# Two chained transformer blocks on one core: moved waits, a reordered opening and first norm, earlier masks, a variance beside a GEMM, the result written by chunk, and a rotary sum moved to POOL

## Chip, cores and metric

One core of one Trainium2 chip runs the whole kernel. The metric is the device time of one execution in microseconds (us), lower is better. The kernel before took 3072.14 us, the median of three runs from 3069.19 to 3078.15.

## What is computed

The input is one sequence of 256 tokens of width 1024 in float32, and the output has the same shape. Two models run one after the other:

```
h = first_block(x, c, ctx, c_ctx, ...)   # 2 layers: FFN, mixer, FFN; each norm scaled and shifted by rows made from c
    layer 0: swiglu(1024 -> 2*2816 -> 1024); retention over x and 256 context tokens; swiglu
    layer 1: swiglu; neighbourhood attention (NAT), 16 heads of 64, bias, softmax over 512 keys; w_o; swiglu
out = second_block(h, ...)               # 2 layers
    proj = rms_norm(x) @ w_in            # 1024 -> queries, keys, values of three attentions, and gates
    oa = rms_norm(diff_attention) * c    # 4 heads, two softmaxes each
    ob = moba_attention                  # 4 heads of 128
    oc = mla_attention                   # 8 heads of 64 + 32 rotary dimensions
    x += rms_norm(sum(sigmoid(gates) * branches) @ w_out)
    x += rms_norm(square(relu(rms_norm(x) @ w_up)) @ w_down)
```

## The kernel before

**Tiling.** Activations stand transposed, channels on the 128 partitions and 256 tokens (512 with the context) along the row. Every weight matrix is streamed from memory once, in blocks of 128 rows by up to 2048 columns per channel group, into six `raw` slots. For float32 accuracy each product is made of three: the weight is split into `w_high`, rounded by ScalarE (ACT, L1004), and `w_low`, the rest, by VectorE (DVE, L1478), and the input into a high and a low half in the same way. TensorE (PE) multiplies high by high, low by high and high by low (L2168). A block is split in two instructions on each engine, and three `w_high` slots exist. A weight block gives one or two chunks of output in PSUM, and four `gemm` banks take them in turn.

**Order.** Nothing is scheduled by a tool. There is one straight program for each engine, and each runs a list of stages of the same names (`ffn`, `norm_in_halves`, `gemm`, `attention`, `update_and_open`). The engines meet at semaphores only. What stands in an engine's queue behind a waiting instruction waits too.

**Attention beside GEMMs.** `attention` is a generator of steps: `scores` (L2320, bias added at L2324), row maximum (DVE, L1702), exponentials (ACT, L1187), division by the sum (DVE, L1721), `turn` (the transposes of the probabilities, L2345 for NAT and L2353 elsewhere, copied out by ACT at L1197 or L1201), and `values` (L2373, out by ACT and DVE at L1207 and L1729). `alongside` sets GEMM chunks between these steps: at step x it has let through `upto` of them. All three engines read the same table:

```python
for x in range(2 * len(a.pairs) + 1):
    next(steps)
    upto = {"nat": min(24, x - x // 13), "dif": (x + 1) // 2, "mob": min(4, 1 + (x + 1) // 2),
            "mla": x + (x + 1) // 2}[a.kind]
```

**Norms.** A norm needs squares (ACT), their sums over partitions by a product with ones (PE, `added_squares` L2093, `mean_square` L2082), a root (ACT), its inverse (DVE, L1510), and the inverse spread over the partitions (PE, L2109). Only then the input of the next GEMM is made (DVE, L1529 and L1516). `norm_in_halves` does it within the last groups of a GEMM (`tail`). `update_and_open` adds a normed output to `h` and opens the next GEMM, and the squares of `h` are taken beside it.

**Queues besides.** SyncE (SP) issues the weight loads in order of use, and POOL has small work: sums of squares (L937), copies of the rotary keys (L974), additions of the branches (L982).

**Names in the rows.** `tt` is the NAT bias with its mask, `mq` and `mk` are the MLA queries and keys, `pexp` the probabilities, `act_high`/`act_low` the split outputs or mixes, `nat_high`/`nat_low` the NAT output, `yt` a temporary, `yh`/`yl` the split normed input. `wide` in `gemm` means that the first two blocks are multiplied row by row of the input as it comes, instead of chunk by chunk.

## Time and profile before

| | us |
|---|---|
| median of 3 runs (lowest, highest) | 3072.14 (3069.19, 3078.15) |
| profiled execution, its own time | 3069.35 |
| its span in the trace | 3067.5 |
| PE busy | 2976.7 |
| DVE busy | 1822.4 |
| ACT busy | 1175.9 |
| POOL busy | 166.7 |

PE is busy for 97% of the span. The mean granted clock of PE was 0.987 of full speed. The rest of the span, 90.8 us, is some fifty waits of PE. In the profile `PE aux L2320 <- ACT pexp L1187` reads: TensorE stood idle before its instruction at line 2320, and what came last of the things it waited for was ScalarE's write of `pexp` at line 1187.

### The profile page before, as it was taken

How to read it: one execution, taken by the hardware profiler on the slowest of the kernel's cores; microseconds unless marked ns; L12 is line 12 of the kernel's file. 1: busy time of each engine (PE TensorE's matmuls, PEld its weight loads, DVE VectorE, ACT ScalarE, POOL GpSimd, SP SyncE). 2: the span in 40 equal slices, each digit the busy share in tenths (PEclk: the TensorE clock that was granted, in tenths of full speed). 3: DMA queues.
4: the chain of work that ended last, by engine and by line, in shares of the span. 5: the costliest groups of instructions: out<-in, count | busy, mean ns of one | idle time of the engine just before them, and what ended most of it. 6: DMA issues, size and time to landing. Idle time of an engine off the chain costs nothing. (4 is left out here: it accounts for less than half of the span.)

```text
span 3067.5 us, 46310 instructions
## 1 busy us (share of the span) xinstructions
PE 2976.7 (97%) x19019; PEld 2647.2 (86%) x19019; DVE 1822.4 (59%) x3378; ACT 1175.9 (38%) x2019; POOL 166.7 (5%) x199
## 2 busy tenths in 40 slices
PE   7999999999999999999999998999999999999998
PEld 4888889888888888888888778999898999899998
DVE  4777775443569886743334445556656656656665
ACT  4222224333342222332223344444544544455453
POOL 2000010000010000100001110000002001001100
PEclk9999999999999999999999999999999999999999
DMA  7556552222236565632324324656335554435452
GB/s 231 151 165 185 158 163 92 73 69 83 69 95 186 185 195 175 194 88 84 110 71 126 92 78 111 186 167 191 97 118 185 165 185 137 138 97 172 152 185 91
DMA packets 509004, 421.42 MB, mean 137 GB/s; under 512 B 18235, under 2 KB 505963, under 8 KB 508793
## 3 DMA queue, kind: packets, MB, share of 16 engines
q1 hardware_dynamic: 505752, 412.33, 43.8%
q0 software_dynamic: 3040, 6.13, 0.8%
q8 instruction: 151, 2.47, 0.3%
q14 instruction: 61, 0.49, 0.1%
HBM read 417.30 MB, written 1.12 MB: 136 GB/s over the span
## 5 line engine op out<-in xcount | busy, mean ns | idle before, releaser
L1478 DVE TENSOR_TENSOR w_low<-raw,w_high 128x1024 fp32r<-128x1024 f32 (+2 forms) x720 | 765.3, 1104 | 321.0 <-ACT w_high L1004 319.8
L1004 ACT ACTIVATE w_high<-raw 128x1024 fp32r<-128x1024 f32 (+2 forms) x720 | 648.6, 950 | 648.6 <-PE gemm L2168 308.1
L2168 PE MATMUL gemm<-xh,w_high 128*128 128x512 f32 (+1 forms) x1904 | 688.4, 362 | 5.1 <-DVE xl L1516 4.5
L2168 PE MATMUL gemm<-xl,w_high 128*128 128x512 f32 (+1 forms) x1904 | 680.9, 358 | 0.0
L2168 PE MATMUL gemm<-xh,w_low 128*128 128x512 f32 (+1 forms) x1904 | 680.8, 358 | 0.0
L2168 PEld LDWEIGHTS gemm<-xh,w_high 128*128 128x128 f32 x1904 | 359.7, 189 | 62.0 <-issue 5.6
L2168 PEld LDWEIGHTS gemm<-xh,w_low 128*128 128x128 f32 x1904 | 359.2, 189 | 57.3
L2168 PEld LDWEIGHTS gemm<-xl,w_high 128*128 128x128 f32 x1904 | 359.6, 189 | 55.5 <-issue 0.2
L2168 PE MATMUL gemm<-yh,w_high 128*128 128x256 f32 x1216 | 350.7, 288 | 12.8 <-DVE yl L1541 7.1
L2168 PE MATMUL gemm<-yl,w_high 128*128 128x256 f32 x1216 | 345.5, 284 | 0.0
L2168 PE MATMUL gemm<-yh,w_low 128*128 128x256 f32 x1216 | 344.9, 284 | 0.0
L1449 DVE SCALAR_TENSOR_TENSOR macc<-raw,sc,macc 128x256 f32<-128x256 f32 x812 | 337.6, 480 | 4.0
L2168 PE MATMUL gemm<-hid_high,w_high 128*128 128x512 f32 (+1 forms) x770 | 272.2, 354 | 0.0
L2168 PE MATMUL gemm<-hid_low,w_high 128*128 128x512 f32 (+1 forms) x770 | 269.1, 350 | 0.0
L2168 PE MATMUL gemm<-hid_high,w_low 128*128 128x512 f32 (+1 forms) x770 | 269.1, 349 | 0.0
L2168 PE MATMUL gemm<-act_high,w_high 128*128 128x256 f32 (+1 forms) x888 | 253.3, 285 | 6.7 <-DVE yt L1671 6.7
L2168 PE MATMUL gemm<-act_low,w_high 128*128 128x256 f32 (+1 forms) x888 | 250.8, 282 | 0.0
L2168 PE MATMUL gemm<-act_high,w_low 128*128 128x256 f32 (+1 forms) x888 | 250.7, 282 | 0.0
L2168 PEld LDWEIGHTS gemm<-yh,w_high 128*128 128x128 f32 x1216 | 232.9, 192 | 16.2 <-issue 14.6
L2168 PEld LDWEIGHTS gemm<-yl,w_high 128*128 128x128 f32 x1216 | 233.0, 192 | 0.2
L2168 PEld LDWEIGHTS gemm<-yh,w_low 128*128 128x128 f32 x1216 | 232.7, 191 | 0.0
L1647 DVE TENSOR_TENSOR hf<-sq,gemm 128x512 f32<-128x512 f32 (+1 forms) x88 | 54.6, 620 | 266.6 <-PE gemm L2168 266.6
(335 smaller groups left out, 4230.1 us busy)
## 6 DMA issues: line engine op xcount, KB each, us to landing
raw<-in_ffn_w_in SPq DMA_DIRECT2D x176, 512.0 KB, 5.2
raw<-in_w_mod SPq DMA_DIRECT2D x72, 1024.0 KB, 7.6
raw<-in_w_in SPq DMA_DIRECT2D x50, 1024.0 KB, 5.3
raw<-in_w_up SPq DMA_DIRECT2D x32, 1024.0 KB, 5.4
raw<-in_w_down SPq DMA_DIRECT2D x32, 1024.0 KB, 5.0
raw<-in_ffn_w_out SPq DMA_DIRECT2D x32, 768.0 KB, 4.6
raw<-in_ret_w_in SPq DMA_DIRECT2D x24, 1024.0 KB, 5.2
raw<-in_ffn_w_out SPq DMA_DIRECT2D x32, 640.0 KB, 4.0
```

The source lines that it names most:

```text
L1004: act.activation(wh[i % SPL][:, a:b], raw[slot_of["w", i]][:, a:b], ACT.Copy).then_inc(w_high, 1)
L1449: dve.scalar_tensor_tensor(out=acc, in0=raw[slot][:, WB * k:WB * k + WB], scalar=sc[:, k, v:v + 1], in1=acc, op0=ALU.mult, op1=ALU.add).th ...
L1478: dve.tensor_tensor(wl[slot][:, a:b], raw[slot][:, a:b], wh[i % SPL][:, a:b].bitcast(F32), ALU.subtract).then_inc(w_low, 1)
L1647: dve.tensor_tensor(hf[:, pr % 2, 0:tok], sa[:, pr % 2, 0:tok], ps[:, 0:tok], ALU.mult).then_inc(odd_free, 1)
L2168: ins = pe.matmul(out, l_, r_, start=first and j == 0, stop=last and j == 2)
```

## The change

These edits are made, none of which changes a number that is computed:

1. **Opening.** SP loads the rows of `x` and `ctx` after three `w_mod` blocks instead of four. PE transposes them before the modulation rows of block 2, and turns and rows of the last blocks stand behind the sums of squares. ACT takes the root, and DVE the inverse, earlier. DVE makes the first two input pieces before the second weight block's low half.
2. **`norm_in_halves`.** In `tail` the sums come 3·nt+2 products into the second half (8 or 14) instead of 6, and the spread 14 or 16 instead of 10.
3. **Masks.** DVE adds the mask to the first four heads' bias ahead of the GEMM `nat_v0` instead of behind it.
4. **`alongside`.** The tables differ by a chunk here and there. MOBA and MLA attention run as one sequence of pairs with one table. The last four steps of NAT let through pieces of the output GEMM `nat_o` on PE, by the new parameter `ahead` (which groups, from which row, to which row).
5. **`mixed{l}`** multiplies rows 0 to 5 of both first blocks, chunk by chunk, before it waits for the last two mixes.
6. **Rotary sums.** The eight additions `mq = yt + yt` of each layer go from DVE (L1990) to POOL, behind the key copies. The MLA scores wait for them, and so do ACT's squares that reuse `yt`.
7. **`update_and_open`.** DVE divides the next piece before it makes the last one's low half, in another order than before for the first two.
8. **Variance.** PE's sums of squares for `mlp_pre` come behind the third group of `up{l}0`, and the squares go to `pexp2` instead of `yt`.
9. **Result.** The final transposes start with each pair of channel groups that is ready, into the four GEMM banks. ACT copies them out in four pieces instead of DVE in eight, and four half-width stores replace two.

```diff
@@ -209,7 +209,7 @@
-        out_buf = [rows_of[:, D * t:D * t + D] for t in range(2)]
+        out_buf = rows_of[:, 0:2 * D].rearrange("p (t n) -> p t n", t=2)
@@ -469,6 +469,8 @@
+            if N["name"][:7] == "mlp_pre":
+                N["buf"] = N["buf"][:3] + (pexp2,)
@@ -775,21 +778,21 @@
-        def alongside(name, steps, rest, lag=0):
+        def alongside(names, steps, rest):
...
-            for x in range(2 * len(a.pairs) + 1):
+            for x in range(2 * sum(len(atts[name].pairs) for name in names) + 1):
...
-                upto = {"nat": min(24, x - x // 13), "dif": (x + 1) // 2, "mob": min(4, 1 + (x + 1) // 2),
-                        "mla": x + (x + 1) // 2}[a.kind]
-                while done < upto - lag:
-                    next(rest)
+                upto = {"nat": min(24, 1 + x - x // 13) + (x >= 28) + (x >= 29) + (x >= 30) + (x >= 32), "dif": min(8, 1 + x // 2),
+                        "mob": min(28, x + 1 + x // 6)}[names[0][:3]]
+                while done < upto:
+                    next(rest, None)
...
+        def pairs_of(names):
+            return [(atts[name], p) for name in names for p in range(len(atts[name].pairs))]
@@ -889,19 +892,20 @@
-            for b in range(4):
+            for b in range(3):
...
-            for b in range(4, len(seq)):
+            for b in range(3, len(seq)):
...
-            for t in range(2):
-                sp.wait_ge(out_rows, 4 * (t + 1))
-                sp.dma_start(A["out"][0, P * t:P * t + P, :],
-                             out_buf[t]).then_inc(out_stored, 16)
-            sp.wait_ge(out_stored, 32)
+            for half_ in range(2):
+                sp.wait_ge(out_rows, 2 * half_ + 2)
+                for t in range(2):
+                    sp.dma_start(A["out"][0, P * t:P * t + P, T2 * half_:T2 * half_ + T2],
+                                 out_buf[:, t, T2 * half_:T2 * half_ + T2]).then_inc(out_stored, 16)
+            sp.wait_ge(out_stored, 64)
@@ -972,6 +976,10 @@
+                pool.wait_ge(roped_part, 4 * l + 4)
+                for hd in range(MH):
+                    g, q = hd // 4, slice(32 * (hd % 4), 32 * (hd % 4) + 32)
+                    pool.tensor_tensor(mq[64:96, hd, :], yt[q, g, :], yt[q, 2 + g, :], ALU.add).then_inc(roped, 1)
@@ -1097,8 +1105,8 @@
-                roots(N)
...
+                    roots(N)
@@ -1254,12 +1262,12 @@
-                if c == 5:
-                    mod_row_out(3)
+                if c in (3, 5):
+                    mod_row_out(c // 2 + 1)
...
+            roots(N)
...
-            roots(N)
@@ -1392,9 +1400,10 @@
+                act.wait_ge(roped, (MH + 1) * (l + 1))
@@ -1408,20 +1417,30 @@
-                alongside(f"moba{l}", attention(f"moba{l}"), gate, 0)
-                alongside(f"mla{l}", attention(f"mla{l}"), both(*(gemm(o, by_chunk=True) for o in with_mla(l))), 0)
+                names = f"moba{l}", f"mla{l}"
+                alongside(names, attention(*names), both(gate, *(gemm(o, by_chunk=True) for o in with_mla(l))))
...
-                    run(gemm(f"up{l}{s}"))
+                    steps = gemm(f"up{l}{s}")
+                    if s == 0:
+                        next(steps)
+                        next(steps)
+                        next(steps)
+                        roots(norms[f"mlp_pre{l}"])
+                    run(steps)
...
+            for k in range(4):
+                act.wait_ge(out_turned, k + 1)
+                act.activation(out_buf[:, :, T * k:T * k + T], bank[k][:, :].rearrange("p (t n) -> p t n", t=2),
+                               ACT.Copy).then_inc(out_rows, 1)
@@ -1553,8 +1575,11 @@
+                    divided(norms[post], c)
+                    if c == 1:
+                        gained_low(N, 0, N["scale"](0, 0))
...
-                    if c:
+                    if c > 1:
@@ -1830,14 +1852,17 @@
+            N = norms["n00"]
+            inverses(N)
...
-            N = norms["n00"]
-            inverses(N)
+            steps = pieces_of(N)
+            next(steps)
+            next(steps)
...
-            run(pieces_of(N))
+            run(steps)
@@ -1948,8 +1973,10 @@
+            for hd in range(4):
+                mask_bias(hd)
@@ -1984,10 +2011,6 @@
-                dve.wait_ge(roped_part, 4 * l + 2 * g + 2)
-                for j in range(4):
-                    q = slice(32 * j, 32 * j + 32)
-                    dve.tensor_tensor(mq[R, 4 * g + j, :], yt[q, g, :], yt[q, 2 + g, :], ALU.add).then_inc(roped, 1)
@@ -2060,11 +2083,8 @@
+                        divided(norms["mlp_post1"], c)
...
-            for t in range(2):
-                for k in range(4):
-                    dve.wait_ge(out_turned, 4 * t + k + 1)
-                    dve.tensor_copy(out_buf[t][:, T * k:T * k + T], aux[k][:, 0:T]).then_inc(out_rows, 1)
@@ -2211,11 +2231,11 @@
-                                    if hf_ and done == 6:
+                                    if hf_ and done == 3 * nt + 2:
...
-                                    if hf_ and done == 10:
+                                    if hf_ and done == (14 if nt == 2 else 16):
@@ -2236,11 +2256,23 @@
+                    for some, r0, r1 in ahead:
+                        for gi in some:
+                            bl, ch = pair[gi]
+                            pe.wait_ge(w_low, 2 * (s + gi) + 2)
+                            for ci in range(len(ch)):
+                                wait_chunk_out(pe, n + 2 * gi + ci - 4)
+                                for k in range(r0, r1):
+                                    if k not in seen:
+                                        x_waits(k)
+                                        seen.add(k)
+                                    products(n + 2 * gi, s + gi, 0, bl, ch, ci, k)
+                        yield 1
...
-                    for k in range(nk):
+                    for k in range(ahead[-1][2] if ahead else 0, nk):
@@ -2295,21 +2327,24 @@
-                    if a.apart or p == 0:
+                    if a.apart or a.kind == "mob" and p == 0:
...
+                    if a.kind == "mla" and p == 0:
+                        pe.wait_ge(roped, (MH + 1) * (a.layer + 1))
+                        pe.wait_ge(kpe_copied, (MH - 1) * (a.layer + 1))
@@ -2420,12 +2455,10 @@
-            mod_rows(2)
-            mod_turn(1)
...
-            mod_turn(2)
+            mod_turn(1)
@@ -2435,16 +2468,18 @@
+            mod_rows(2)
...
+            mod_turn(2)
+            add_partitions(MOD0 + 1)
...
-            add_partitions(MOD0 + 1)
-            mod_rows(5)
-            mod_turn(4)
...
+            mod_turn(4)
+            mod_rows(5)
@@ -2519,9 +2554,10 @@
-            alongside("nat", attention("nat"), both(*(gemm(f"nat_{k}{g}", by_chunk=True) for g in range(1, 4) for k in "qkv")))
-            pe.wait_ge(o_low, atts["nat"].p1)
-            run(gemm("nat_o"))
+            last = gemm("nat_o", lambda kc: pe.wait_ge(o_low, 2 * kc + 2), wide=True,
+                        ahead=(((0,), 0, 5), ((1,), 0, 5), ((0, 1), 5, 6), ((0, 1), 6, 7)))
+            alongside(("nat",), attention("nat"),
+                      both(*(gemm(f"nat_{k}{g}", by_chunk=True) for g in range(1, 4) for k in "qkv"), last))
@@ -2535,12 +2571,15 @@
-                        added_squares(norms[pre])
-                        for x in norms[pre]["own"]:
-                            mean_square(norms[pre], x)
-                        if pre == "mix_pre1":
-                            spread(norms[pre])
+                        sums(pre)
+                        spread(norms[pre])
...
+            def sums(name):
+                added_squares(norms[name])
+                for x in norms[name]["own"]:
+                    mean_square(norms[name], x)
@@ -2612,32 +2652,39 @@
-                alongside(f"moba{l}", behind_subln(attention(f"moba{l}")), gate)
-                pe.wait_ge(kpe_copied, (MH - 1) * (l + 1))
-                pe.wait_ge(sub_low, DH * (l + 1))
-                pe.wait_ge(o_low, atts[f"moba{l}"].p1)
-                alongside(f"mla{l}", attention(f"mla{l}"), both(*(gemm(o, by_chunk=True) for o in with_mla(l))))
+                names = f"moba{l}", f"mla{l}"
+                inputs = {f"branch0{l}": lambda kc: pe.wait_ge(sub_low, DH * (l + 1)), f"gate1{l}": None,
+                          f"branch1{l}": lambda kc: pe.wait_ge(o_low, atts[f"moba{l}"].p1)}
+                alongside(names, behind_subln(attention(*names)),
+                          both(gate, *(gemm(o, inputs[o], by_chunk=True) for o in with_mla(l))))
...
-                run(gemm(f"mixed{l}", lambda kc: pe.wait_ge(mix_low, 8 * l + kc + 1), wide=True))
+                run(gemm(f"mixed{l}", lambda kc: pe.wait_ge(mix_low, 8 * l + kc + 1), wide=True,
+                         ahead=(((0, 1), 0, DC - 2),)))
...
-                    run(gemm(f"up{l}{s}", lambda kc: pe.wait_ge(x_low, pre["p0"] + kc + 1), wide=s == 0,
-                             after_row=opened(f"mlp_pre{l}")))
+                    steps = gemm(f"up{l}{s}", lambda kc: pe.wait_ge(x_low, pre["p0"] + kc + 1), wide=s == 0)
+                    if s == 0:
+                        next(steps)
+                        next(steps)
+                        next(steps)
+                        sums(f"mlp_pre{l}")
+                    run(steps)
...
-            pe.wait_ge(h_update, 8 + 32)
-            for t in range(2):
-                for k in range(4):
-                    if t:
-                        pe.wait_ge(out_rows, k + 1)
+            up = norms["mlp_post1"]["up0"]
+            for k in range(4):
+                wait_chunk_out(pe, G["down13"].n0 + 4 + k)
+                pe.wait_ge(h_update, up + 2 * k + 2)
+                for t in range(2):
...
-                        ins = pe.transpose(aux[k][:, P * c:P * c + P], h[:, 2 * k + c, P * t:P * t + P], ident)
-                    ins.then_inc(out_turned, 1)
+                        at = T * t + P * c
+                        ins = pe.transpose(bank[k][:, at:at + P], h[:, 2 * k + c, P * t:P * t + P], ident)
+                ins.then_inc(out_turned, 1)
```

The order of instructions shows three places. In them `[waits ...]` names the semaphores that an instruction waits for, and each row is the first of a run of products.

PE at the start of `mixed0` (two blocks of two chunks, eight rows). Before:

```order
L2168 MATMUL gemm<-act_high,w_high 128x256 [waits even_chunk_out,odd_chunk_out,mixed_low_ready,w_low_ready]
L2168 MATMUL gemm<-act_high,w_high 128x256 [waits mixed_low_ready]
L2168 MATMUL gemm<-act_high,w_high 128x256 [waits mixed_low_ready]
L2168 MATMUL gemm<-act_high,w_high 128x256 [waits mixed_low_ready]
L2168 MATMUL gemm<-act_high,w_high 128x256 [waits mixed_low_ready]
```

Now:

```order
L2188 MATMUL gemm<-act_high,w_high 128x256 [waits mixed_low_ready,even_chunk_out,w_low_ready]
L2188 MATMUL gemm<-act_high,w_high 128x256 [waits mixed_low_ready]
L2188 MATMUL gemm<-act_high,w_high 128x256 [waits odd_chunk_out]
L2188 MATMUL gemm<-act_high,w_high 128x256 [waits even_chunk_out,w_low_ready]
L2188 MATMUL gemm<-act_high,w_high 128x256 [waits odd_chunk_out]
L2188 MATMUL gemm<-act_high,w_high 128x256 [waits even_chunk_out,odd_chunk_out,mixed_low_ready,w_low_ready]
L2188 MATMUL gemm<-act_high,w_high 128x256 [waits mixed_low_ready]
```

Before, each row of the input had 12 products behind its own wait. Now 72 products over rows 0 to 5 stand ahead of the wait for row 6.

PE at the start of the differential attention of layer 0. Before:

```order
L2320 MATMUL aux<-diff_qk_gate 128x128 [waits t5_loaded,even_chunk_out,h_updated,odd_chunk_out,probs_ready,rope_done]
L2320 MATMUL aux<-diff_qk_gate 128x128
L2324 MATMUL aux<-t,cst 128x128 x2
L2320 MATMUL aux<-diff_qk_gate 128x256 [waits probs_ready]
L2320 MATMUL aux<-diff_qk_gate 128x256
L2324 MATMUL aux<-t,cst 128x256 x2
L2168 MATMUL gemm<-yh,w_high 128x256 [waits even_chunk_out,w_low_ready]
L2353 MATMUL aux<-cst,pexp 128x128 [waits turned_probs_out,probs_divided]
```

Now:

```order
L2355 MATMUL aux<-diff_qk_gate 128x128 [waits t5_loaded,h_updated,even_chunk_out,odd_chunk_out,probs_ready,rope_products,rope_done]
L2355 MATMUL aux<-diff_qk_gate 128x128
L2359 MATMUL aux<-t,cst 128x128 x2
L2188 MATMUL gemm<-yh,w_high 128x256 [waits even_chunk_out,w_low_ready]
L2355 MATMUL aux<-diff_qk_gate 128x256 [waits probs_ready]
L2355 MATMUL aux<-diff_qk_gate 128x256
L2359 MATMUL aux<-t,cst 128x256 x2
L2388 MATMUL aux<-cst,pexp 128x128 [waits turned_probs_out,probs_divided]
```

The GEMM chunk (24 products) moved from behind the second scores, which wait for the first pair's exponentials, to ahead of them. The first scores wait for the rotary products and one rotary piece, no longer for the sums.

PE at the end of NAT attention. Before, with nothing of `nat_o` until the last values:

```order
L2345 MATMUL aux<-cst,sq 128x128 [waits turned_probs_out,probs_divided]
L2345 MATMUL aux<-cst,sq 128x128 x3
L2345 MATMUL aux<-cst,sq 128x128 [waits turned_probs_out,probs_divided]
L2345 MATMUL aux<-cst,sq 128x128 x3
L2373 MATMUL aux<-xt,nv 64x128 [waits attention_high_ready,attention_low_ready,turned_probs_out]
L2373 MATMUL aux<-xt,nv 64x128 x7
L2168 MATMUL gemm<-nat_high,w_high 128x256 [waits even_chunk_out,w_low_ready,attention_low_ready]
```

Now:

```order
L2380 MATMUL aux<-cst,sq 128x128 [waits turned_probs_out,probs_divided]
L2380 MATMUL aux<-cst,sq 128x128 x3
L2188 MATMUL gemm<-nat_high,w_high 128x256 [waits attention_low_ready,even_chunk_out,w_low_ready]
L2188 MATMUL gemm<-nat_high,w_high 128x256 [waits odd_chunk_out]
L2188 MATMUL gemm<-nat_high,w_high 128x256 [waits even_chunk_out,w_low_ready]
L2188 MATMUL gemm<-nat_high,w_high 128x256 [waits odd_chunk_out]
L2408 MATMUL aux<-xt,nv 64x128 [waits attention_high_ready,attention_low_ready,turned_probs_out]
L2408 MATMUL aux<-xt,nv 64x128 x7
L2188 MATMUL gemm<-nat_high,w_high 128x256 [waits even_chunk_out,odd_chunk_out,attention_low_ready,w_low_ready]
L2188 MATMUL gemm<-nat_high,w_high 128x256 [waits even_chunk_out,w_low_ready]
```

Twelve products of `nat_o` (row 6 of both first blocks) now stand between the last turn and the last values. Rows 0 to 5 stand further ahead in the same way, and only row 7, twelve products, is left before the third block.

## Rows read from the trace of the kernel before

**Rows 1.** The page: the span and part 1 (busy us, share, instructions).

```profile
span 3067.5 us, 46310 instructions
PE 2976.7 (97%) x19019; PEld 2647.2 (86%) x19019; DVE 1822.4 (59%) x3378; ACT 1175.9 (38%) x2019; POOL 166.7 (5%) x199
```

**Rows 2.** Waits of PE, whole span: total us, times, longest us.

```profile
PE aux L2320 <- ACT pexp L1187: 7.8, 3, 3.0
PE aux L2639 <- DVE h L1547: 7.0, 1, 7.0
PE gemm L2168 <- DVE yt L1671: 6.7, 2, 3.4
PE aux L2373 <- ACT hf L1201: 3.3, 4, 1.0
PE aux L2373 <- ACT turned L1201: 3.1, 5, 0.8
PE gemm L2168 <- DVE hf L1656: 2.7, 2, 1.3
PE aux L2320 <- DVE tt L1738: 2.6, 2, 1.5
PE aux L2093 <- POOL sq L937: 2.3, 1, 2.3
PE aux L2320 <- DVE act_low L1729: 2.3, 2, 1.1
PE aux L2320 <- DVE mq L1990: 1.5, 2, 0.9
```

**Rows 3.** Windows: us, busy PE, PEld, DVE, ACT, POOL; clock, DMA share, GB/s.

```profile
2350.00:2370.00 20.00, 20.00 (x172) 20.00 (x170) 11.68 (x16) 8.20 (x14) 6.24 (x5) 1.00 0.49 158
2345.40:2348.70 3.30, 3.30 (x17) 3.30 (x17) 0.85 (x2) 2.90 (x5) 0.75 (x2) 0.50 0.39 129
2731.10:2734.40 3.30, 3.30 (x14) 3.03 (x13) 0.77 (x3) 0.81 (x4) 0.00 (x0) 0.50 0.00 0
2240.00:2308.00 68.00, 64.75 (x537) 61.28 (x536) 42.61 (x90) 33.83 (x84) 5.18 (x7) 1.00 0.45 139
```

**Rows 4.** Timeline of PE: start, us, line, operation, [idle before <-releaser].

```profile
61.31 0.77 PE L2168 MATMUL gemm<-xh,w_high 128*128 128x512 f32 x1 [2.63 <-DVE xl L1516]
...
1858.24 1.09 PE L2373 MATMUL aux<-hf,nv 128*64 128x128 f32 x16 [0.75 <-ACT hf L1197]
...
1864.21 0.39 PE L2168 MATMUL gemm<-nat_high,w_high 128*128 128x256 f32 x1 [0.70 <-DVE nat_low L1729]
```

**Rows 5.** Timeline of ACT and DVE behind the last NAT values.

```profile
1863.85 1.28 ACT L1114 ACT_TABLE_LOAD   x1
1865.25 1.99 ACT L1004 ACTIVATE w_high<-raw 128x1024 fp32r<-128x1024 f32 x2
...
1866.43 2.36 DVE L1478 TENSOR_TENSOR w_low<-raw,w_high 128x1024 fp32r<-128x1024 f32 x2 [2.27 <-ACT w_high L1004]
```

**Rows 6.** Timeline of DVE, rotary sums and low halves ahead of differential attention.

```profile
2152.22 2.10 DVE L1990 TENSOR_TENSOR mq<-yt 32x256 f32<-32x256 f32 x4
2154.35 2.64 DVE L1478 TENSOR_TENSOR w_low<-raw,w_high 128x1024 fp32r<-128x1024 f32 x2
...
2158.36 1.76 DVE L1990 TENSOR_TENSOR mq<-yt 32x256 f32<-32x256 f32 x4
```

**Rows 7.** POOL by lines: busy us, mean ns, idle before.

```profile
L982 POOL TENSOR_TENSOR h<-h,yt 128x256 f32<-128x256 f32 x32 | 23.8, 762 | 357.6 <-DVE yt L1671 357.6
L974 POOL COPY mk<-mk 32x256 f32<-32x256 f32 x14 | 8.9, 682 | 126.2 <-DVE mk L1980 126.2
```

**Rows 8.** Timeline of the end: PE, DVE and SP.

```profile
3060.34 3.67 PE L2639 MATMUL aux<-cst,h 128*128 128x128 f32 x16 [6.99 <-DVE h L1547]
...
3061.06 3.41 DVE L2067 COPY t<-aux 128x256 f32<-128x256 f32 x8 [0.78 <-PE aux L2639]
...
3062.80 2.06 SPq L902 DMA_DIRECT2D out<-t  x2
```

More of the change, by code:

```diff
@@ L574, in add_att @@
             a.nat = a.kind == "nat"
+            a.layer = 0 if a.nat else int(name[-1])
             a.apart = a.kind in ("nat", "dif")
@@ L1175, in gemm, with attention, exponentials @@
                             yield 1
-            def attention(name):
-                a = atts[name]
-                n = len(a.pairs)
-                def exponentials(p, i):
+            def attention(*names):
+                pairs = pairs_of(names)
+                n = len(pairs)
+                def exponentials(a, p, i):
                     g = a.p0 + p
@@ L1360, in _ @@
             run(gemm("nat_v0"))
-            alongside("nat", attention("nat"), both(*(gemm(f"nat_{k}{g}", by_chunk=True) for g in range(1, 4) for k in "qkv")))
+            alongside(("nat",), attention("nat"), both(*(gemm(f"nat_{k}{g}", by_chunk=True) for g in range(1, 4) for k in "qkv")))
             run(gemm("nat_o"))
@@ L1950, in _ @@
             run(gemm("nat_qk0"))
+            for hd in range(4):
+                mask_bias(hd)
             run(gemm("nat_v0"))
-            alongside("nat", attention("nat"), both(*(gemm(f"nat_{k}{g}", by_chunk=True) for g in range(1, 4) for k in "qkv")))
+            alongside(("nat",), attention("nat"), both(*(gemm(f"nat_{k}{g}", by_chunk=True) for g in range(1, 4) for k in "qkv")))
             run(gemm("nat_o"))
@@ L2024, in _ @@
                 run(steps)
-                alongside(f"diff{l}", attention(f"diff{l}"), both(*(gemm(o, by_chunk=True) for o in with_diff(l))), 0)
+                alongside((f"diff{l}",), attention(f"diff{l}"), both(*(gemm(o, by_chunk=True) for o in with_diff(l))))
                 gate = gemm(f"gate0{l}", by_chunk=True)
@@ L2376, in values @@
                     ins.then_inc(o_ready, 1)
-                scores(0)
+                scores(*pairs[0])
                 yield 1
-                for p in range(n):
-                    if p + 1 < n:
-                        scores(p + 1)
-                    if p:
-                        values(p - 1)
-                    turn(p, 0)
+                for j, (a, p) in enumerate(pairs):
+                    if j + 1 < n:
+                        scores(*pairs[j + 1])
+                    if j:
+                        values(*pairs[j - 1])
+                    turn(a, p, 0)
                     yield 1
-                    turn(p, 1)
+                    turn(a, p, 1)
                     yield 1
-                values(n - 1)
+                values(*pairs[n - 1])
             pe.wait_ge(consts_in, 16)
@@ L2583, in _ @@
                 wait_gemm_out(pe, f"diff_v{l}1")
-                alongside(f"diff{l}", attention(f"diff{l}"), both(*(gemm(o, by_chunk=True) for o in with_diff(l))))
+                alongside((f"diff{l}",), attention(f"diff{l}"), both(*(gemm(o, by_chunk=True) for o in with_diff(l))))
                 gate = gemm(f"gate0{l}", by_chunk=True)
```

103 lines of the change are left out of this document (50 added, 53 removed).

## The prediction

> **What bounds the kernel.** I read the page first, then the waits of PE, the timeline at each longer wait, and the windows around them. PE is busy for 2976.7 of 3067.5 us [rows 1]. VectorE comes next with 1822.4, so over the whole kernel only PE is a bound, and what can be won without less PE work is its 90.8 us of waiting and the time at the lower clock. The waits of PE name the places [rows 2], and nearly all the large ones are touched by the change. The windows give the second cost. At full clock PE does 172 instructions in 20 us, 0.116 us each. Just behind the waits at 2345.25 and 2730.80 it ran at a granted clock of 0.50, the lower of its two levels (1.2 of 2.4 GHz), though it was busy throughout [rows 3]. Sixteen stretches of the trace read so, 3.4 us long or a multiple. At half speed one costs half its length, 1.7 us. By counting (17 instructions in 3.3 us instead of 28) it is 1.3, so a removed stretch is worth 1.3 to 1.7 and I take 1.7.
>
> Durations are from the profiled execution, whose own time is 3069.35 us. That is 2.8 under the median of 3072.14.
>
> **1. Starts of the three attentions: 8.5 us.** The first pair's exponentials are waited for three times, 7.8 us [rows 2]: 1.8 for NAT and 3.0 for each differential attention. In the new order a GEMM chunk of 24 products, 24 x 0.116 = 2.8 us of PE work, stands there. The mask, 1.5 of the 2.6 us on `tt` (the longest of two), goes too, since its four additions now run beside `nat_v0`. So do the 1.5 us on `mq`, whose sums leave DVE, and two of the four waits on `hf`, 0.6 each. Together 12.0, and three stretches of low clock, 5.1. The covering work brings new waits. The chunk's weights are split first, so the division of the first pair stands behind two low halves of 1.1 to 1.3 us each on DVE [rows 6], and the first turn waits for the division. Row maximum, exponentials and division take about 2.4 us, which with 2.3 for the low halves is 4.7 against 2.8 of cover: up to 1.9 us, where the low halves do not run earlier. I take 0.9 for NAT, and for each differential attention 1.5 there and 3 x 0.8 at every second turn, where chunk and turn changed places: 8.6 in all. 12.0 + 5.1 - 8.6 = 8.5. Bounds: 2.4 (new waits cost the clock as well) and 16 (none comes).
>
> **2. End of NAT: -2.0 us.** The last two pairs now wait for 6.1 us in seven places: 1.1 of the mask [rows 2], 0.75 and 0.70 shown in [rows 4], and four more of 0.84 to 1.02. The pieces of `nat_o` fill half of them, and 3.2 remain. But little is then left for later. Before, 96 products (11 us) covered the third block's split. Now only row 7 is left, 12 products or 1.4 us. ACT must write the last `nat_high`, load a table (1.28) and make `w_high` (1.99), and DVE's `w_low` ends at 1868.79, 4.9 us after the last values' output [rows 5]. That is a new wait of some 3.5 us, and by the windows a drop of the clock (1.4 of its 1.7 counted). 6.1 - 3.2 - 3.5 - 1.4 = -2.0, an edit that loses. Bounds: -2.4 and +4.5 (the split runs earlier than the queue reads).
>
> **3. MOBA and MLA as one sequence: 7.6 us.** At the hand-over PE waits 1.0 for `hf`, 0.8 for `turned` and 1.1 for `act_low`, in both layers [rows 2], 5.8 in all. The next scores now need no drained pair. One stretch of low clock, the one at 2731.1 [rows 3], goes as well, 1.7. Bounds 5 and 9.
>
> **4. First rows of `mixed`: 10.0 us.** PE waits 6.7 us on `yt` in two layers [rows 2], each time followed by low clock, 3.4 in all. Seventy-two products, 8.4 us, now stand between. Rows 6 and 7 of the input are ready some 2 us behind the end of the wait, long before PE comes to them. Bounds 9 and 10.4.
>
> **5. Variance beside `up`: 2.6 us.** The 2.7 us on `hf` of L1656 [rows 2] come from the root, whose sums stood two groups earlier. They now stand behind a further group, and the first `relu` no longer waits for them. Bounds 2.0 and 2.7. **`update_and_open`**: the first low half comes one addition sooner, 0.2 x 3 = 0.6 (0 to 1). The wait of 2.37 on `yl` stays.
>
> **6. Opening and `norm_in_halves`: 0.** The input rows land about 3 us sooner, but PE had modulation work in that time, and the same products remain. From the spread to the first GEMM PE waited 2.63 us [rows 4], because two low halves ran before the first input piece. They now stand behind the second piece, and PE has too few products by then, so the wait splits and does not go: -0.3 (-2 to +3). In `ret_out3` the 2.3 us on POOL's squares [rows 2] go, but the later spread moves the root behind the next `w_high`, and I expect a wait as long: +0.3 (-0.5 to +2.3). The other tails have no wait and get none.
>
> **7. Rotary sums: 0.** DVE loses 16 additions, 2.10 and 1.76 us for four [rows 6]. POOL gains 16. The nearest rows are its copy of the same shape, 682 ns, and its addition of 128x256, 762 ns [rows 7]: 5.8 us a layer, up to 11 at the price of its slower sums. The MLA scores and ACT's squares need them some 45 us later, and POOL's next work later still. The cover is the whole differential attention, and without it the price would be 5.8 us a layer. DVE may be slowed: two low halves took 2.64 us beside POOL's copies where 2.36 is usual [rows 5, 6]. That is 0.3 us, off PE's path.
>
> The Trainium skill, page "SBUF — State Buffer", section on its two separate sides, goes further: VectorE with two operands in SBUF and GpSimd share a port pair as an exclusive lock, held for a whole instruction. By that rule the subtractions of `w_low` and the POOL sums would stand in line. The 2.64 us agree with some delay, not with a full one.
>
> **8. The end: 2.2 us.** PE waits 7.0 us for the last of eight updates [rows 2], then come 3.67 us of transposes (at low clock) and copies that end at 3064.5 (3061.06 + 3.41), and the last store ends the span 3.0 us later [rows 8]. Now three of four pairs are transposed and copied while updates run. Behind the last update (3060.3) stand 4 transposes (0.9, a quarter of 3.67), one copy of four times 128x128 (0.8 by two of DVE's 0.43), and the store with its second issue (3.2): 3065.2 for 3067.5. Bounds 1.5 and 3.5.
>
> The sum: 8.5 - 2.0 + 7.6 + 10.0 + 2.6 + 0.6 + 0 + 2.2 = 29.5. 3069.35 - 29.5 = 3039.9, and with about half of what the median stands above the profiled execution, **3041 us**.
>
> The Trainium skill, page "TensorE: Matmul & The Clock Gate", prices low clock as its length times one minus the ratio of clocks, which is the 1.7 taken here. By the count [rows 3], 1.3 a stretch, the sum would be 2.4 smaller for six stretches, 27.1.
>
> **Rivals.**
> - *The new waits do not come.* DVE is idle for a third of most stretches, and low halves may run early. Parts 1 and 2 then give 16 and 3, part 8 gives 3: 42, about 3029. For it speaks that my queue reading takes every split as late as it can be. Against it, waits of 0.84 at each turn exist already.
> - *Freed time turns into waits at the turns.* DVE stands behind low halves at each step, the clock falls again, and parts 1, 2, 3 and 6 give 1, -2.4, 5 and -2.5. With the lower bounds elsewhere about 15 is left, 3056. PE is busy for 64.75 of 68 us and DVE for 42.61 in the MLA stretch [rows 3], so there is room, which speaks against it.
> - *The port pair locks fully.* Sixteen sums hold DVE for 11.6 us near the start of attention, where the first chunks need their low halves. On PE's path it takes 29.5 to 18, 3052. The Trainium skill's page on SBUF states this lock; the 0.3 us above speak against it.
> - *The releaser named was not the only one.* Waits reappear behind the next semaphore a little later, in parts 3, 4 and 5. Then 8 is left, 3063.
> - *Slower.* The merged stretch is one mechanism. In its 24 steps GEMM chunks come at a fixed rate of one a step, each with its splits in front of the division. If VectorE were late by over 0.8 us a step in both layers, 48 x 0.8 = 38 us would be lost, more than the rest gives (22): 3088. It decides from 0.5 us a step. VectorE would have to be over 100% busy with the same work that takes 63% now [rows 3].
>
> **How the numbers follow.** Forecast 0.64; no new waits 0.13; waits at the turns 0.12; locked ports 0.03; another releaser 0.05; slower 0.03. All bounds at their ends together would give 3016 to 3054, which is unlikely for eight parts. 8 in 10 lie between 3027 and 3057, which takes in the first three cases. A measurement can tell 0.3%, 9.2 us, so faster means under 3062.9: the first four cases, 0.92. The releaser case lies at that border, 0.05, and slower has 0.03.
>
> **What would show it.** Right: no wait over 1 us at the starts of the attentions and none ahead of `mixed`; a new wait of 3 to 4 us before the third block of `nat_o`, with low clock behind it; ten or eleven stretches of low clock instead of sixteen; L1656 gone from the waits; POOL 12 us busier, VectorE 7 less; the last update followed by 5 us instead of 7. Wrong: VectorE releasing PE at the turns for over 1 us each, PE waiting for POOL's sums, or an opening that differs by over 3 us.

## The result and the profile after

The changed kernel takes 3054.24 us, the median of four runs from 3052.89 to 3055.26. The kernel before took 3074.24 beside it, and 3074.76 over the thirteen runs of the whole study (3068.67 to 3077.58). The ratio is 0.9936, with a 95% interval from 0.9918 to 0.9953. That is faster by 0.6%, inside the range of 3027 to 3057, but with a gain of 20 us where some 30 were forecast.

First the page of the changed kernel, its span and part 1, then its waits of PE: total us, times, longest us.

```profile
span 3051.8 us, 46326 instructions
PE 2972.0 (97%) x19019; PEld 2642.8 (87%) x19019; DVE 1812.9 (59%) x3354; ACT 1174.7 (38%) x2023; POOL 184.9 (6%) x215
```

```profile
PE aux L2388 <- issue: 7.7, 8, 2.3
PE gemm L2188 <- DVE xl L1535: 6.8, 2, 5.0
PE aux L2388 <- DVE pexp L1750: 5.1, 8, 1.5
PE aux L2408 <- ACT hf L1209: 3.9, 4, 1.4
PE gemm L2686 <- DVE h L1569: 3.8, 4, 2.0
PE gemm L2188 <- DVE h L1660: 3.4, 1, 3.4
PE gemm L2188 <- issue: 2.5, 1, 2.5
PE aux L2388 <- DVE pexp L1754: 2.3, 2, 1.2
PE aux L2408 <- ACT turned L1209: 1.1, 2, 0.6
PE gemm L2188 <- DVE hf L1681: 0.4, 2, 0.2
```

The waits for exponentials, the mask, `mq`, the last mixes and POOL's squares [rows 2] are gone, and L1656's 2.7 us on `hf` are 0.4. New are 12.8 us in front of L2388, the turn of the differential attention (for half of them the profile names "issue", no releaser), 3.4 before the third block of `nat_o`, 5.0 before the first product (2.63 before, [rows 4]), and 2.5 at 897 us behind the norm of `ret_out3`, where POOL's squares had cost 2.3. VectorE is busy for 9.5 us less and POOL for 18.2 more, where I had written 7 and 12.

Both kernels issue 19019 matmuls, so the start of the same product can be set side by side in the two timelines. This is the difference by stage, gained us positive:

| stage | gained | forecast |
|---|---|---|
| to the first GEMM product | -4.2 | -0.3 |
| `ret_out3` and its norm | +0.9 | +0.3 |
| FFN up to NAT | +0.9 | 0 |
| start of NAT | +4.5 | +4.1 |
| middle of NAT | -0.5 | 0 |
| end of NAT and `nat_o` | -1.9 | -2.0 |
| differential attention, layers 0 and 1 | -1.4, -1.4 | +2.4, +2.0 |
| MOBA and MLA, layers 0 and 1 | +2.0, +3.1 | +7.6 for both |
| `mixed`, layers 0 and 1 | +5.2, +5.1 | +5.0, +5.0 |
| norms to `up` and the MLP, both layers | +1.9 | +3.2 |
| input of layer 1 | -0.7 | 0 |
| the end | +2.3 | +2.2 |
| sum | 15.8 | 29.5 |

The spans differ by as much, 3067.5 - 3051.8 = 15.7 us. The medians differ by 4 us more, because the profiled execution of before, 3069.35, was among its fastest.

### The profile page after: what moved, and what is told of

Read it like the earlier page. It is cut to its first block, busy times and chain, and to the rows that moved or that the text cites. A ratio compares the mean times of both kernels' runs of the same rounds, so it can differ in the third digit from the quotient of the medians.

```text
span 3051.8 us, 46326 instructions
## 1 busy us (share of the span) xinstructions
PE 2972.0 (97%) x19019; PEld 2642.8 (87%) x19019; DVE 1812.9 (59%) x3354; ACT 1174.7 (38%) x2023; POOL 184.9 (6%) x215
## 4 chain that ended last, share of the span: by engine, by line
PE 94%; DVE 3%; ACT 1%; issue 1%; DMA 0%; SPq 0%; DVEq 0%; ACTq 0%
PE gemm L2188 84%; PE aux L2150 1%; PE aux L2516 1%; PE aux L2359 1%; PE aux L2355 1%; PE aux L2408 1%; DVE w_low L1497 1%; PE aux L2539 1%; PE aux L2102 1%; PE aux L2380 1%; PE gemm L2439 1%; ACT w_high L1012 1%; PE aux L2129 0%; PE aux L2388 0%; DMA raw<-in_w_mod 0%
## 5 line engine op out<-in xcount | busy, mean ns | idle before, releaser
L2188 PEld LDWEIGHTS gemm<-xh,w_high 128*128 128x128 f32 x1904 | 361.4, 190 | 65.5 <-issue 10.0
```

The lines of the kernel that those rows point to most:

```text
L2188: ins = pe.matmul(out, l_, r_, start=first and j == 0, stop=last and j == 2)
```

## Experiments

**The opening put back.** The edit, and the same for ACT's, DVE's and PE's order:

```diff
-            for b in range(3):
+            for b in range(4):
                 load_block(b)
```

> The changed kernel with the opening alone put back (load order, modulation rows of block 2 before the transposes, turns, root and low halves as before). Theory, the new order costs: before the change PE did the 3.6 to 5.3 us of modulation rows of block 2 while it waited for the input, and now it does them later, so the first GEMM product moves from 65.5 back to about 61.3 us in the trace and the time falls by 4 us, to about 3050. Rival, the 4 us are a matter of where the low clock falls in this one profile: then the first GEMM stays within 1 us of 65.5 or the gain is gone at the end of the first FFN, and the time stays at 3054.

It took 3051.11 us (3049.68 to 3052.3), 3.1 less than the changed kernel. Its first product began at 64.00. These are the timelines of the changed kernel, PE and DVE (start, us):

```profile
53.03 5.30 PE L2439 MATMUL gemm<-raw,sc 128*2 128x256 f32 x16
...
59.33 1.16 PE L2129 MATMUL aux<-cst,inv 128*128 128x128 f32 x8
65.46 0.76 PE L2188 MATMUL gemm<-xh,w_high 128*128 128x512 f32 x1 [4.98 <-DVE xl L1535]
```

```profile
60.60 0.87 DVE L1548 SCALAR_TENSOR_TENSOR xt<-h,nsc,aux 128x256 f32<-128x256 f32 x2 [0.59 <-PE aux L2129]
61.39 2.35 DVE L1497 TENSOR_TENSOR w_low<-raw,w_high 128x1024 fp32r<-128x1024 f32 x2
63.66 0.47 DVE L1548 SCALAR_TENSOR_TENSOR xt<-h,nsc,aux 128x256 f32<-128x256 f32 x1
64.05 0.48 DVE L1535 SCALAR_TENSOR_TENSOR xl<-xt,mod,xh 128x256 fp32r<-128x256 f32 x1
```

and of e1:

```profile
59.27 2.08 PE L2126 MATMUL aux<-cst,inv 128*128 128x128 f32 x8 [0.88 <-DVE inv L1529]
64.00 0.77 PE L2185 MATMUL gemm<-xh,w_high 128*128 128x512 f32 x1 [2.66 <-DVE xl L1535]
```

The two early pieces are `xt`. The first `xl` is made one step later, so it stands behind both low halves all the same, and those 2.35 us are now in the open (4.98 for 2.66). Before, they ran beside the spread. The start scatters by some us from one execution to the next. Five traces of the new order, the changed kernel and four experiments that keep it, have their first product at 65.5, 69.4, 70.1, 63.5 and 65.1, a mean of 66.7. (The two late ones, e2 and e3, waited 3.5 and 4.4 us for a `w_mod` block where the others waited 2.4.) Eight of the old order (before, e1, e5 to e9 and e12) lie from 61.3 to 64.0, with a mean of 62.9. So the order costs about 3.8 us, which one trace could not have shown. The wait itself does not scatter: it is 4.98 in all five and 2.6 to 2.7 in all eight. The rest of the 3.8, after the wait of 0.9 for `inv` that the new order saves, was not taken apart.

**The table of the differential attention put back.**

```diff
-"dif": min(8, 1 + x // 2)
+"dif": (x + 1) // 2
```

> The changed kernel with the table of the differential attention alone put back to (x + 1) // 2; the sums stay on POOL. Theory A, the table: a chunk behind the turn instead of ahead of it leaves the division uncovered, so the small waits of 0.35 to 0.7 at seven turns and the 1.47 at the last one come from it; they vanish (4.3 us a layer), the wait of 3.0 for the first exponentials and about 0.6 come back with low clock (1.7), and the stretch gets shorter by some 1 us a layer: about 3052. Theory B, the sums on POOL slow VectorE: the waits at the turns stay, and the time grows by 2 to 4 us.

It took 3043.33 us (3042.48 to 3044.94), 10.9 less than the changed kernel. Theory A holds, and the gain is much larger than it expected (3043 for 3052). From the start of the attention to the hand-over the changed kernel loses 1.4 us a layer against before, and this one gains 4.6 and 4.5. Two lines of PE's timeline in e2, and then of the changed kernel:

```profile
2165.48 0.70 PE L2355 MATMUL aux<-diff_qk_gate 64*128 64x256 f32 x4 [1.00 <-ACT pexp L1195]
...
2169.92 0.27 PE L2388 MATMUL aux<-cst,pexp 128*128 128x128 f32 x1
```

```profile
2167.41 0.30 PE L2388 MATMUL aux<-cst,pexp 128*128 128x128 f32 x1 [2.28 <-issue]
2172.18 0.44 PE L2388 MATMUL aux<-cst,pexp 128*128 128x128 f32 x2 [0.35 <-DVE pexp L1750]
2178.30 0.30 PE L2388 MATMUL aux<-cst,pexp 128*128 128x128 f32 x1 [0.71 <-issue]
```

With the old table the chunk stands between the scores and the turn, and the turn waits for nothing. With the new one it stands behind the turn. VectorE takes the chunk's output first and the division after it, and PE comes to the turn with only the scores as cover. So it waits at all eight turns of layer 0: 2.28, 0.35, 0.71, 0.35, 0.51, 0.40, 0.50 and 1.47, together 6.6 us. The wait for the first exponentials, 3.0 us before, came back as 1.0 only. That was the surprise, and e8 explains it.

**POOL's sums later.**

```diff
                 pool.wait_ge(roped_part, 4 * l + 4)
+                pool.wait_ge(p_ready, 2 * atts[f"diff{l}"].p0 + 6)
```

> The changed kernel with one more wait on POOL: the eight sums start after the third pair's exponentials. Theory, VectorE's low halves took 1.75 us each beside these sums and 1.22 without them, and that lengthens the wait at the first turn (2.28 and 1.95 us): it falls to about 1.2 in both layers, low halves at the start take 1.22, and the time falls by 2 us. Rival, the low halves are slow for another reason (the DMA of weights in that stretch): they stay at 1.75 and so does the wait. A second possibility: the same slowing appears at the fourth pair, as a wait there of up to 1 us, and nothing is won.

It took 3056.26 us (3053.13 to 3058.55), no better than the changed kernel. VectorE's low halves in the changed kernel, and in e3 first without and then beside the sums:

```profile
2162.62 3.43 DVE L1497 TENSOR_TENSOR w_low<-raw,w_high 128x1024 fp32r<-128x1024 f32 x2 [1.70 <-ACT w_high L1012]
```

```profile
2167.19 2.36 DVE L1498 TENSOR_TENSOR w_low<-raw,w_high 128x1024 fp32r<-128x1024 f32 x2 [1.70 <-ACT w_high L1013]
...
2178.09 3.02 DVE L1498 TENSOR_TENSOR w_low<-raw,w_high 128x1024 fp32r<-128x1024 f32 x2 [2.06 <-ACT w_high L1013]
```

And PE's turns in e3:

```profile
2170.91 0.30 PE L2389 MATMUL aux<-cst,pexp 128*128 128x128 f32 x1 [1.22 <-issue]
...
2182.74 0.30 PE L2389 MATMUL aux<-cst,pexp 128*128 128x128 f32 x1 [1.64 <-issue]
```

The slowing is the sums' doing. The first wait fell from 2.28 to 1.22 as expected, and the third grew from 0.71 to 1.64: wherever the sums run beside a pair of low halves, up to 1.1 us are lost. The second possibility of the expectation is what happened.

**One chunk first, then the old order, with late sums.** The table was `1 if x < 3 else (x + 1) // 2`.

> The changed kernel with late sums and a table that lets one chunk through behind the first scores and the others ahead of the turns as before the change (1 if x < 3 else (x + 1) // 2). If the covers are as theory A has them, the first wait is about 1.2, the seven small ones and the 1.47 go, 0.6 and 0.56 remain: 4 to 5 us less in each layer than in the changed kernel, about 3046. If VectorE is the bound in this stretch, the waits move elsewhere in it and less than 1.5 us a layer is won.

It took 3048.32 us (3042.86 to 3050.2) with the new opening, 5 more than e2. The small waits are gone. But the stretch won 3.3 us in layer 0 and 1.4 in layer 1 against before, less than e2's 4.6 and 4.5 (the runs scatter over 7 us, so the stages say more than the median): a chunk ahead of the first turn brings its low halves ahead of the first division (1.2 us), and the second scores then wait for their exponentials as well (1.0). It was a worse repair than the old table. How much of layer 1's loss is due to the late sums was not separated.

**Opening and table put back together.**

> The changed kernel with both the opening and the table of the differential attention put back (e1 and e2 together). e1 was 3 us and e2 11 us under the changed kernel. If the two are independent the time is 3040 to 3041. If the opening's difference in e1 was only the scatter of the first 60 us from execution to execution (the first GEMM began at 65.5, 64.0, 69.4, 70.1 and 63.5 in the traces so far, though three of these kernels open alike), the time stays at 3043.

It took 3038.85 us (3036.17 to 3039.83), 4.5 under e2. The two add, as far as the scatter lets one see. This is the base of what follows.

**The third block of `nat_o` split early.**

```diff
-both(*(gemm(f"nat_{k}{g}", by_chunk=True) for g in range(1, 4) for k in "qkv"))
+both(*(gemm(f"nat_{k}{g}", by_chunk=True) for g in range(1, 4) for k in "qkv"), once(splits_upto, G["nat_o"].s0 + 2))
```

`once` does the call at step 28, on ACT and on DVE.

> e5 with one edit: ACT and DVE split the third weight block of the output GEMM of NAT attention beside its last pairs, not behind them. Theory: the wait of 3.4 us ahead of that block in the changed kernel is the split, late since too little of the first two blocks is left to cover it; it goes, and the time falls by 3 us against e5. Rival: ACT's two microseconds stand ahead of the last turns' copies instead, and the waits there grow by as much: 0 to 1 us won.

It took 3034.33 us (3033.36 to 3034.8), 4.5 under e5. In the changed kernel, PE and then ACT behind the last values:

```profile
1874.52 0.36 PE L2188 MATMUL gemm<-nat_high,w_high 128*128 128x256 f32 x1 [3.38 <-DVE h L1660]
```

```profile
1869.04 1.28 ACT L1122 ACT_TABLE_LOAD   x1
1870.34 0.20 ACT L1122 ACTIVATE spare_root<-eps 128x1 f32<-128x1 f32 x1
1870.45 3.88 ACT L1012 ACTIVATE w_high<-raw 128x1024 fp32r<-128x1024 f32 x4
```

The windows of the same 13 us, in e5 and then in e6 (us, busy PE, PEld, DVE, ACT, POOL; clock):

```profile
1864.30:1877.30 13.00, 9.59 (x66) 9.44 (x67) 10.39 (x12) 8.76 (x13) 4.32 (x3) 0.87 0.63 162
```

```profile
1867.00:1880.00 13.00, 12.94 (x110) 12.97 (x110) 10.82 (x13) 9.27 (x15) 6.27 (x5) 1.00 0.94 237
```

PE does 110 instructions instead of 66. The wait is gone and this window is at full clock, and ACT's two halves cost nothing at step 28: no wait at the last turns is longer. The low clock did not go for good. e5 has 3.4 us of it at 1870.7 and 3.4 at 1887.8, at the next norm; e6 has 6.8 at 1882.7, around that norm, and gives 0.7 of its 5.1 us back there. That the late split makes the wait, as part 2 of the forecast has it, is shown.

**Two chunks at the end of the merged sequence.**

```diff
-"mob": min(28, x + 1 + x // 6)
+"mob": (21, 22, 22, 23, 25, 27, 28)[min(x - 18, 6)] if x > 17 else x + 1 + x // 6
```

> e5 with another table at the end of the merged MOBA and MLA sequence: from step 18 on 21, 22, 22, 23, 25, 27, 28 chunks instead of 22, 23, 24, 25, 26, 27, 28, so that two short chunks stand ahead of the last values and the last turn. Theory: the waits of 1.35 and 1.15 us there come from single chunks of 12 products (1.7 us) as cover; both go to under 0.3 and some 0.5 comes at step 20: 1.5 to 2 us less a layer, 3 to 4 in all against e5. Rival: the copies and divisions there are late behind ACT's and DVE's splits of these same chunks, which come later too: the sum of the waits stays within 0.5 us a layer.

It took 3037.15 us (3036.34 to 3038.96), 1.7 under e5 with overlapping ranges. The traces give 0.5 us a layer. In e5, then in e7:

```profile
PE aux L2405 <- ACT hf L1209: 5.2, 6, 1.4
PE aux L2385 <- DVE pexp L1754: 2.3, 2, 1.1
```

```profile
PE aux L2405 <- ACT hf L1209: 2.4, 4, 0.6
PE aux L2385 <- DVE pexp L1754: 3.6, 4, 1.6
```

The wait for `hf` goes and the one for the division grows, so the rival was mostly right: the division stands behind the splits of the chunk that was to cover it. In both layers that pair of low halves also ran beside two POOL additions and took 3.3 us instead of e5's 2.36, so about 1 of the new wait of 1.6 is the slowing that e3 shows.

**The rotary sums back on VectorE.** The loop over `mq` moved from POOL to `rope_queries` on DVE.

> e5 with the rotary sums back on VectorE, ahead of the differential attention, in its old place in the queue (PE's own wait for them stays at the MLA scores). Theory: what freed the start of the differential attention is this move, since eight sums of 0.46 us stood in VectorE's queue ahead of the low halves and the first row maxima; the wait for the first exponentials goes back from 1.0 to 3.0 us with low clock behind it, and the time grows by 4 us a layer, 7 to 8 in all. Rival: PE no longer waiting for the sums at the first scores is what counted: then the time stays within 2 us of e5.

It took 3049.47 us (3049.19 to 3051.11), 10.6 over e5. In e8, PE and the window behind it:

```profile
2161.26 1.23 PE L2351 MATMUL aux<-diff_qk_gate 64*128 64x256 f32 x4 [3.96 <-ACT pexp L1191]
```

```profile
2159.00:2165.60 6.60, 4.34 (x15) 3.33 (x16) 3.27 (x10) 1.98 (x9) 0.00 (x0) 0.50 0.30 104
```

The wait of 1.00 is 3.96, as much as before's 3.0 for the exponentials and 0.9 for `mq` together, and the low clock returns. By stage the move is worth 4.9 us a layer, with the old table in place (with the new one it was not run). Of the gains that were measured alone it is the largest beside `mixed`, and the forecast priced it at the 1.5 us on `mq` alone.

**Both repairs.** e6 and e7 together.

> e6 and e7 together (opening and differential table back, third block split early, more chunks at the end of the merged sequence). The two touch different stretches, so their gains over e5 should add: 4.5 and 1.1 by the traces (1.7 by the medians), about 3033.

It took 3032.73 us (3032.46 to 3035.14), as expected.

**The first two modulation rows written out earlier.** In ACT's queue `mod_row_out(0)` and `mod_row_out(1)` stand ahead of the decays.

> e9 with one edit: ACT writes out the first two modulation rows before it works on the decays and lambdas, not behind them. Theory: PE's wait of 3.4 to 3.8 us at 26 us is for this queue, since the first rows' products are done by 22 us; it goes, the transposes start 3 us earlier (the input has landed by 27) and the first GEMM with them: 3 us less than e9. Rival: the input's landing or the later modulation blocks set the pace, and the wait moves to the transposes or the rows of blocks 3 to 5: under 1 us won.

It took 3031.50 us (3029.93 to 3033.49), the fastest of the study, 0.9863 of before (0.9848 to 0.9878). Against e9 it is 1.2 us, within the scatter. In e10:

```profile
23.37 0.60 PE L2455 MATMUL gemm<-cst,mrow 2*128 2x2 f32 x4
...
31.00 0.60 PE L2455 MATMUL gemm<-cst,mrow 2*128 2x2 f32 x4 [2.00 <-ACT mrow L1252]
31.54 5.38 PE L2474 MATMUL aux<-cst,xrows 128*128 128x128 f32 x32
37.66 1.05 PE L2155 MATMUL aux<-ones,macc 128*128 128x1 f32 x8 [0.74 <-ACT h L1267]
```

The wait at 26 us is gone. Two of its 3.2 us came back at 31.00, ahead of the transposes, as a wait for the third row, which ACT writes behind the same work. The low clock then fell on the transposes (5.38 us for 3.72). The rival was nearer.

**`mixed` put back.** Without `ahead=(((0, 1), 0, DC - 2),)`.

> The changed kernel with the first rows of mixed alone put back (no products ahead of the wait for rows 6 and 7). Theory: the wait of 3.4 us on VectorE's last mixes and the 3.4 us of low clock behind it come back in both layers, 5.0 us each by the row of before: 10 us more than the changed kernel, 3064. Rival: since other waits ahead of it moved, the low clock may not fall there, and only 6.7 us come back: 3061.

It took 3067.20 us, the median of ten runs (3065.01 to 3069.39), 13.0 over the changed kernel and above both expectations (3064 and 3061). In e11, the wait and the two windows behind it:

```profile
2344.60 0.55 PE L2188 MATMUL gemm<-act_high,w_high 128*128 128x256 f32 x1 [3.42 <-DVE yt L1696]
```

```profile
2343.60:2350.30 6.70, 5.70 (x27) 5.73 (x28) 3.35 (x7) 4.21 (x6) 1.42 (x2) 0.50 0.39 127
2831.70:2838.40 6.70, 6.09 (x28) 6.12 (x29) 3.35 (x6) 4.21 (x6) 1.42 (x2) 0.50 0.32 109
```

The waits are the 6.7 us of before to a tenth, but here each low stretch is 6.8 us long, twice that of before. The products behind the wait come 6.2 and 6.6 us later.

**MOBA and MLA apart**, on e6.

> e6 with MOBA and MLA attention as two sequences again, each with its own table as before the change. Theory: merging won the hand-over (2.9 us of waits a layer) and gave some back at the end, where 1.35 and 1.15 us are waited for instead of 0.5 and 0.9: with the two apart the hand-over comes back and the end gets shorter, 1.9 to 3 us a layer more than e6, 4 to 6 in all: about 3039. Rival: the hand-over waits are filled by other queue positions now, and the time stays within 1 us of e6.

It took 3037.85 us (3036.72 to 3038.95), 3.5 over e6. By stage 2.7 us a layer come back at the hand-over, and 2.0 are won at the end. Merging is worth about 0.9 us a layer by the traces; the rest of the 3.5 lies in stretches that the edit does not touch, 1.2 of it ahead of the differential attention. The expectation's mechanism holds, its size was too high. Of the 5.1 us that the two stages gained against before, some 3.2 stay with the two apart: the wait on `act_low` (1.1 a layer) and the low clock of layer 1 at 2731 [rows 3] do not come back. By the code that is the moved waits for the inputs of `branch0` and `branch1`, which now stand at those GEMMs and not ahead of the MLA scores; no run puts them back alone.

The start of NAT, the variance beside `up`, `update_and_open`, the later sums in `norm_in_halves` and the end were never taken out alone. For these parts there are the stages of the table and the waits, one trace of each kernel.

## Why the forecast was right and where it was wrong

The time lies in the stated range, 3 us from its slow end, and the sign held. Most parts came out near their price, but the sum owes some luck to two errors in the differential attention that partly cancel. Of the 13.7 us that the sum was too high, 11.1 lie in two places, the differential attention (7.2) and the opening (3.9).

- **Part 4, `mixed`:** right. 10.3 us by stage for 10.0. e11 shows that it hangs on the clock: 10 to 13.
- **Part 2, end of NAT:** right in sign, size and cause, -1.9 for -2.0. The wait of 3.4 stood where the queue put it (3.5), and e6 removes it. Only the low clock fell elsewhere: none behind this wait in the changed kernel's trace, but 6.8 us instead of 3.4 at the norm 15 us later, which cost the 1.4 that was counted.
- **Part 8, the end:** right, 2.3 for 2.2.
- **Part 1, NAT:** right, 4.5 for 4.1, with a new wait of 0.92 at the first turn (0.9).
- **Part 1, differential attention:** wrong, -2.8 for +4.4, and this is the largest miss. The step that failed is "1.5 there and 3 x 0.8 at every second turn". I counted low halves ahead of a division and left out that the chunk's own output also stands there, at every turn, and that the last turn had lost its chunk altogether. The waits at the turns are 6.6 us, not 3.9. e2 puts the table's cost at 6 us a layer.
- **Part 7, rotary sums: 0:** wrong. They stood ahead of the first row maxima on VectorE, so they were in the chain of the wait for the exponentials. I credited its removal to the table. e8 shows 4.9 us a layer for the sums. The two errors lie in one place. Of the +4.4 there, 1.5 (the waits on `mq`) were for the sums and 2.9 for the table. With the sums moved and the old table the stretch gained 9.1 (e2), and the new table then lost 12: 7.6 too low and 14.9 too high, so the stretch came out only 7.2 too high.
- **Part 6, opening: 0:** wrong, -4.2, beyond my bound of -2 to +3. I had written that the wait "splits and does not go". It grew by 2.35, since nothing of `xl` came ahead of the low halves. The norm of `ret_out3` gave 0.9, near its 0.3, and there a wait of 2.5 took the place of 2.3, as I had expected.
- **Part 3, merging:** the waits of the hand-over went as forecast and the size was off, 5.1 for 7.6. By e12 merging itself gives 1.9 of it, and the rest stays without it, by the code through the moved waits for `branch0` and `branch1`. Waits of 1.35 and 1.15 at its end were not in the sum, as only one short chunk a step is left there.
- **Part 5:** L1656's 2.7 us went down to 0.4, but the stage won 1.9 for 3.2, and why is open.
- **Signs:** ten stretches of low clock, no wait ahead of `mixed` and 5.0 us behind the last update came as written. Not as written were 2.3 and 1.9 us at the first turns of the differential attentions, VectorE 9.5 us less busy (7) and POOL 18.2 more (12), since its sums took up to 1.65 us each. One sign of being wrong came: the opening differs by over 3 us.
- **Sums:** some terms do not add up to what I wrote. Part 1's new waits are 0.9 + 2 x 3.9 = 8.7 (8.6), part 3 is 5.8 + 1.7 = 7.5 (7.6), part 8's terms give 2.3 (2.2). The rival of waits at the turns has 13.6 left by its own bounds, 3057, and not 15.

Of the rivals, *freed time turns into waits at the turns* is what the opening and the differential attention did, and its 3056 is nearer to 3054.24 than my 3041. It had 0.12. It let parts 1, 2, 3 and 6 give 1, -2.4, 5 and -2.5, and by stage they gave 1.7, -1.9, 5.1 and -3.3. But it had the clock fall at the turns too, and in the changed kernel no stretch of low clock lies between 1897 and 2367 us. Part 1 gave no more than 1.7 because the sums' 9 us did not make up for the table's 12.

## What to carry to other kernels

When an interleaving table is shifted by one step, write out for each waiting instruction what now stands ahead of its producer in that producer's own queue. A chunk is cover only between the producer's start and the wait, and its output and splits are a load on the same queue. Before pricing a moved operation at nothing, ask whether it stood ahead of the first link of a chain that is waited for. An edit made of nine parts should be measured with parts taken out: here a gain of 20 us held losses of 11 (the table), 3 to 4.5 (the opening) and 4.5 (the late third block).

## What the runs showed of the hardware

POOL additions of 32x256 that read two operands in SBUF took 0.72 us when VectorE was idle. Beside `w_low` subtractions they took about 1.6, and two of these took 3.43 us instead of 2.36. The whole group:

```profile
2156.79 9.85 POOL L982 TENSOR_TENSOR mq<-yt 32x256 f32<-32x256 f32 x8 [0.36 <-DVE yt L2013]
```

Taking turns whole would make each subtraction 1.18 + 0.72 = 1.9 us, and 1.72 was measured, so it is nearly that. I had said that the 2.64 us of [rows 6] showed some delay but not a full one. The Trainium skill, page "SBUF — State Buffer", section on its two separate sides, says that the engine that comes second is blocked for the whole instruction, and these numbers agree with it better than my reading did. The rival of locked ports, with 11.6 us on PE's path, still did not come: some 1.1 us a layer reached PE (e3). The same happened beside POOL's branch additions of 128x256 in e7, 3.3 us for two low halves.

The low clock followed waits in lengths of 3.4 or 6.8 us for the same wait in the same place. Behind the 3.4 us at `mixed` it was 3.4 in before's trace and 6.8 in e11's. In all 77.0 us of before's span were at the lower clock and 66.1 of the changed kernel's. Its ten stretches for sixteen were therefore worth about 5 us at half speed, and not the 10 that I had counted for six, since eight of the ten are 6.8 us or longer, while twelve of before's sixteen are 3.4.
